# Rows of a routed layer fetched and stored by DMA through DRAM instead of one-hot products on TensorE, for seven of eight experts

## The reference

```python
N_EXPERTS_2, D_FF_EXPERT, TOP_K = 8, 3584, 2

def moe_swiglu(x, w_router, w_gate, w_up, w_down):
    logits = (x @ w_router).astype(jnp.float32)
    top_val, top_idx = lax.top_k(logits, TOP_K)
    top_w = jax.nn.softmax(top_val, axis=-1)
    gate = jnp.einsum('bsk,bske->bse', top_w,
                      jax.nn.one_hot(top_idx, N_EXPERTS_2, dtype=jnp.float32)).astype(x.dtype)
    y = jnp.zeros_like(x)
    for e in range(N_EXPERTS_2):
        h = jax.nn.silu(x @ w_gate[e]) * (x @ w_up[e])
        y = y + gate[..., e:e + 1] * (h @ w_down[e])
    return y

# second_block, layer i = 1, its last lines
ff = moe_swiglu(h, moe_w_router[j], moe_w_gate[j], moe_w_up[j], moe_w_down[j])
h = layer_norm(ALPHA_2 * h + ff, ln_g[i, 2], ln_b[i, 2])
```

## Time and profile before

| | us |
|---|---|
| median of three runs | 2299.82 (2298.18 to 2302.2) |
| the profiled execution | 2297.7 |
| its span (first to last instruction) | 2295.9 |
| the second routed layer, about 1256 to 2281 in the trace | 1025 |
| one expert within it | 125.6 |

### The profile page before, as it was taken

The page is one execution under the profiler, slowest core; times in us unless marked ns, Lnnn a source line. Parts: engine busy times, 40 slices in busy tenths (PEclk is TensorE's granted clock), DMA queues, the critical chain, the costliest instruction groups (busy, mean ns, idle before and its releaser), DMA issues.

```text
span 2295.9 us, 31086 instructions
## 1 busy us (share of the span) xinstructions
PE 2154.6 (94%) x12260; PEld 1728.6 (75%) x12260; DVE 1556.2 (68%) x1913; ACT 1226.8 (53%) x1352; POOL 127.4 (6%) x123
## 2 busy tenths in 40 slices
PE   8998899999988889999987999999999999999996
PEld 8886883443876879987676788888888888888885
DVE  4557661222556676763477888888888988888886
ACT  4554431111335454433555777776777777777773
POOL 2112000000000023330000000000000000000000
PEclk9998999999989999998999999999999999999998
DMA  8640649999452344567113899999999999999994
GB/s 268 185 147 3 191 177 385 417 417 408 144 170 86 103 164 165 168 194 183 65 56 129 306 369 332 366 334 363 347 351 346 352 355 347 367 330 367 335 368 155
DMA packets 285709, 592.02 MB, mean 258 GB/s; under 512 B 12155, under 2 KB 118031, under 8 KB 277280
## 3 DMA queue, kind: packets, MB, share of 16 engines
q1 hardware_dynamic: 280016, 571.54, 69.9%
q0 software_dynamic: 5584, 19.00, 2.7%
HBM read 589.39 MB, written 1.11 MB: 257 GB/s over the span
## 4 chain that ended last, share of the span: by engine, by line
PE 84%; DVE 6%; ACT 4%; DMA 3%; issue 2%; POOL 0%; SPq 0%; DVEq 0%; ACTq 0%
PE psF L1137 12%; PE psF L1139 12%; PE psF L1138 12%; PE psB L1137 9%; PE psB L1138 9%; PE psB L1139 9%; PE psF L1554 4%; PE psB L1576 2%; PE psB L1416 1%; PE psB L1599 1%; PE psF L1380 1%; PE psB L1211 1%; PE psF L1585 1%; DVE ring_rounded L2269 1%; PE psB L1219 1%
## 5 line engine op out<-in xcount | busy, mean ns | idle before, releaser
L2664 DVE TENSOR_TENSOR ring_rounded<-ring,arena_rounded 128x2048 fp32r<-128x2048 f32 x226 | 512.0, 2286 | 31.2 <-ACT arena_rounded L2009 30.1
L2009 ACT ACTIVATE arena_rounded<-ring 128x2048 fp32r<-128x2048 f32 x226 | 433.7, 1920 | 168.9 <-DMA ring<-in_moe_w_up_dram 108.5
L1137 PE MATMUL psF<-arena_rounded 128*128 128x512 f32 x896 | 358.1, 400 | 3.6 <-ACT arena_rounded L2031 1.6
L1139 PE MATMUL psF<-arena_rounded 128*128 128x512 f32 x896 | 354.3, 395 | 0.0
L1138 PE MATMUL psF<-ring_rounded,arena_rounded 128*128 128x512 f32 x896 | 352.9, 394 | 0.0
L2269 DVE TENSOR_TENSOR ring_rounded<-ring,ring_rounded 128x2048 fp32r<-128x2048 f32 (+1 forms) x71 | 154.0, 2170 | 171.0 <-ACT ring_rounded L1837 170.6
L1137 PEld LDWEIGHTS psF<-arena_rounded 128*128 128x128 f32 x896 | 168.8, 188 | 43.4 <-issue 5.0
L1139 PEld LDWEIGHTS psF<-arena_rounded 128*128 128x128 f32 x896 | 168.5, 188 | 39.1
L1138 PEld LDWEIGHTS psF<-ring_rounded,arena_rounded 128*128 128x128 f32 x896 | 168.7, 188 | 37.5
L1138 PE MATMUL psB<-ring_rounded,PT_rounded 128*128 128x512 f32 x448 | 177.0, 395 | 0.0
L1837 ACT ACTIVATE ring_rounded<-ring 128x2048 fp32r<-128x2048 f32 (+1 forms) x71 | 128.6, 1813 | 85.4 <-PE psF L1139 62.7
(11 more groups left out here) (453 smaller groups left out, 4532.3 us busy)
## 6 DMA issues: line engine op xcount, KB each, us to landing
ring<-in_moe_w_gate_dram SPq DMA_DIRECT2D x112, 1024.0 KB, 5.2
ring<-in_moe_w_up_dram SPq DMA_DIRECT2D x112, 1024.0 KB, 5.2
ring<-in_moe_w_down_dram SPq DMA_DIRECT2D x112, 1024.0 KB, 4.9
ring<-in_w_dram SPq DMA_DIRECT2D x48, 1024.0 KB, 16.7
arena<-in_w_dram SPq DMA_DIRECT2D x16, 1024.0 KB, 19.1
ring<-in_w_in_dram SPq DMA_DIRECT2D x14, 1024.0 KB, 5.3
ring<-in_ff_w_gate_dram SPq DMA_DIRECT2D x11, 1024.0 KB, 7.4
ring<-in_ff_w_up_dram SPq DMA_DIRECT2D x11, 1024.0 KB, 9.8
```

Of the source, the lines that this page charges most:

```text
L1137: mm(bank, x1, w1, start=start, stop=False, skip_group_check=open_groups)
L1139: return mm(bank, x2, w1, start=False, stop=stop, skip_group_check=open_groups)
L2009: ap_(w_hi[slot].bitcast(R32), ring[:, slot], ACT.Copy).then_inc(q["high"], 1)
L2664: V.tensor_tensor(ring_r[:, slot].bitcast(R32), ring[:, slot], w_hi[slot], ALU.subtract)\
```

## The change

For all units of round 0 (`direct` is true when the layer is split and the round is the number 0):
- The tokens `h` are written to DRAM once (1 MB). DVE computes for each token the numbers of its two slots (`number_rows`, step 3 of unit 0) and its gates (`gates_of_rows`, step 4). POOL scatters the token numbers to a table in DRAM with four indirect DMAs and reads it back as one column per expert.
- For units 1 to 7 POOL brings the rows with one indirect DMA of 128 rows of 4 KB into `xg_rows2`. PE's `gather` and ACT's `rows` are left out for them. `turn_rows` stands ahead of the last `down` of a unit instead of in its middle, and the halves of the rows (`slots`) come between the first and the second weight chunk on ACT and on DVE.
- For units 0 to 6 ACT copies the result without its gate (`y_save`) and POOL stores it to DRAM (0.5 MB each). `marks`, `y_high`, `y_low`, `scatter` and their sums are left out for them.
- In unit 7 POOL brings back, for each half of the tokens, two rows per token (four indirect DMAs of 0.5 MB), and DVE adds them with their gates in steps 3 and 5 (`add_rows`). Unit 7's own result goes the old way by `marks`, `y_high`, `y_low`, `scatter`.
- The counts on which semaphores are awaited are adapted, and two columns join the constants.

```diff
+        y_rows = Region(13824).get(D)
+        n_back = E2 - 1
+        tokens_dram = nc.dram_tensor("routed_tokens", (T, D), F32, kind="Internal").ap()
+        y_dram = nc.dram_tensor("expert_rows", (n_back * SLOTS, D), F32, kind="Internal").ap()
...
+            moe2 = layers["moe2"]
+            pool.wait_ge(numbers_ready, 1)
+            pool.dma_start(token_of[0:E2 * SLOTS].rearrange("(p e) a -> p (e a)", p=P), no_token).then_inc(blanked, 16)
+            pool.wait_ge(moe2.q["tokens_dve"], 1)
+            pool.dma_start(tokens_dram.rearrange("(t p) d -> p t d", p=P), h[:]).then_inc(tokens_out, 16)
+            pool.wait_ge(numbers_ready, 2)
+            pool.wait_ge(blanked, 16)
+            for k in range(2):
+                for t in range(TT):
+                    i = TT * k + t
+                    pool.indirect_dma_start(token_of, bass.IndirectOffsetOnAxis(slot_no[:, i:i + 1], 0), own_no[:, t:t + 1], None)\
+                        .then_inc(numbers_out, 16)
+            pool.wait_ge(numbers_out, 16 * 2 * TT)
+            pool.dma_start(token_no, token_of[0:E2 * SLOTS].rearrange("(e s) a -> s (e a)", s=SLOTS),
+                           allow_slow_non_contiguous=True).then_inc(numbers_back, 16)
+            pool.wait_ge(numbers_back, 16)
+            pool.wait_ge(tokens_out, 16)
+            def store_rows(u):
+                pool.wait_ge(y_saved, 2 * u + 2)
+                pool.dma_start(y_dram[SLOTS * u:SLOTS * u + SLOTS], y_rows).then_inc(y_out, 16)
+            for u in range(1, E2):
+                pool.wait_ge(moe2.q["slots_ready"], 2 * u)
+                pool.indirect_dma_start(xg_rows2, None, tokens_dram, bass.IndirectOffsetOnAxis(token_no[:, u:u + 1], 0))\
+                    .then_inc(rows_in, 16)
+                if u >= 2:
+                    store_rows(u - 2)
+            store_rows(n_back - 1)
+            pool.wait_ge(y_out, 16 * n_back)
+            pool.wait_ge(moe2.q["slots_ready"], 2 * E2)
+            for t in range(TT):
+                if t:
+                    pool.wait_ge(back_added, t)
+                for k in range(2):
+                    i = TT * k + t
+                    pool.indirect_dma_start(back_rows[:, k], None, y_dram, bass.IndirectOffsetOnAxis(back_no[:, i:i + 1], 0))\
+                        .then_inc(back_in, 16)
...
                 def down(u, s, n, where, next_rows=None):
                     pe.wait_ge(q["turned_dve" if layer.split else "turned_act"], steps_done + n)
-                    if s == 0:
-                        past(q["y_dve"], 2 * units_done + 2 * u)
+                    if s == 0 and direct:
+                        past(y_saved, 2 * u)
+                    elif s == 0:
+                        past(q["y_dve"], 2 * layer.written(r, u))
                     for j in range(2):
                         if j == 1 and next_rows is not None:
                             turn_rows(next_rows)
...
                 def turn_rows(u):
                     rows_ = xg_rows1 if per == 1 else xg_rows2
+                    brought = direct and not (isinstance(u, int) and u == 0)
+                    if brought:
+                        pe.wait_ge(rows_in, u * 16)
                     for a in range(2):
-                        pe.wait_ge(q["rows_saved"], (units_done + u) * 2 + 2)
+                        if not brought:
+                            pe.wait_ge(q["rows_saved"], layer.gathers(r, u) * 2 + 2)
                         for k in range(4):
...
-                    scattered = per == 1 and (isinstance(u, int) and u >= 2) or per > 1 and s == 1 and not begin
+                    scattered = per == 1 and (isinstance(u, int) and u >= 2) or per > 1 and s == 1 and not begin and not direct
                     if not begins:
-                        if s == 2:
+                        if s == 2 and not direct:
                             pe.wait_ge(q["added"], layer.adds(r, u, 0))
                         elif per == 1 and (u >= 2 or not (isinstance(r, int) and r == 0)):
                             pe.wait_ge(q["added"], layer.adds(r, u - 2, 0))
                         out_of = u - 1 if per > 1 else u - 2
                         scatter(out_of, steps_done + n)
                     gate_up(n, 1, 1, where)
-                    if per == 1 and not begin or per > 1 and s == 1:
+                    if per == 1 and not begin or per > 1 and s == 1 and (end or not direct):
                         mine = u if per > 1 else u - 1
                         if scattered:
                             pe.wait_ge(q["added"], layer.adds(r, out_of, 1))
                         marks(mine)
-                    if s == per - 1 and not end:
+                    if s == per - 1 and not end and not direct:
                         gather(u + 1, layer.adds(r, out_of, 3) if scattered else None)
                     next_rows = u + 1 if s == per - 1 and not end else None
+                    if direct and next_rows is not None:
+                        turn_rows(next_rows)
+                        next_rows = None
                     if not begins:
                         down(u if s else u - 1, (s - 1) % per, n, where, next_rows)
                     elif next_rows is not None:
...
+                def y_save(u, n, where):
+                    act.wait_ge(q["used"], layer.nth(layer.every, r, n, 6 * layer.group - 1, where))
+                    for c in range(2):
+                        ap_(y_rows[:, 512 * c:512 * c + 512], Y[c][:, :], ACT.Copy).then_inc(y_saved, 1)
                 def unit(u, begin, end):
                     for s in range(per):
                         step(u, s, begin and s == 0, end and s == per - 1, end)
+                    if direct and not begin:
+                        act.wait_ge(y_out, u * 16)
...
+                    switch = s == per - 1 and not end
                     if layer.split and not ends:
                         high(n + 1, 0)
+                    if switch and direct:
+                        slots(u + 1)
+                    if layer.split and not ends:
                         high(n + 1, 1)
-                    if s == per - 1 and not end:
+                    if switch and not direct:
                         rows(u + 1)
                     if layer.split and not ends:
                         high(n + 1, 2)
-                    if s == per - 1 and not end:
+                    if switch and not direct:
                         slots(u + 1)
                     if layer.split and not ends:
                         high(n + 1, 3)
                     if s == 0 and not begins:
-                        y_high(u - 1, n, where)
+                        (y_save if direct else y_high)(u - 1, n, where)
...
+                def number_rows():
...
+                    V.tensor_scalar(own_no, spare_row, -float(E2 * SLOTS + 1), None, ALU.add)
+                    do(V.tensor_scalar(slot_base, const("iota")[:, 0:E2], float(SLOTS), 1.0, ALU.mult, ALU.add))
+                    do(V.tensor_tensor(ids, slot, slot_base.unsqueeze(1).broadcast_to([P, TT, E2]), ALU.add))
+                    do(V.scalar_tensor_tensor(out=ids, in0=slot, scalar=SLOTS - 0.5, in1=ids, op0=ALU.is_lt, op1=ALU.mult))
...
+                    do(V.scalar_tensor_tensor(out=pairs(none_of), in0=pairs(two_ids), scalar=0.5,
+                                              in1=spare_row.unsqueeze(1).broadcast_to([P, 2, TT]), op0=ALU.is_lt, op1=ALU.mult))
+                    V.scalar_tensor_tensor(out=slot_no, in0=two_ids, scalar=-1.0, in1=none_of, op0=ALU.add, op1=ALU.add)
+                    V.tensor_scalar(back_no, two_back, -1.0, 0.0, ALU.add, ALU.max).then_inc(numbers_ready, 1)
...
+                def gates_of_rows():
...
+                    some, own = gates[:, :, 0:n_back], same[:, :, 0:n_back]
+                    V.tensor_reduce(gate_sum, some, AX.X, ALU.add)
+                    do(V.tensor_tensor(own, ids[:, :, 0:n_back], two_back[:, 0:TT].unsqueeze(2).broadcast_to([P, TT, n_back]), ALU.is_equal))
+                    do(V.tensor_tensor(own, own, some, ALU.mult))
+                    do(V.tensor_reduce(back_gate[:, 0:TT], own, AX.X, ALU.add))
+                    do(V.tensor_tensor(back_gate[:, TT:2 * TT], gate_sum, back_gate[:, 0:TT], ALU.subtract))
...
+                def add_rows(t):
+                    part = acc_of[layer.name][:, t]
+                    dve.wait_ge(q["added"], CREDIT)
+                    dve.wait_ge(back_in, 32 * t + 32)
+                    for k in range(2):
+                        i = TT * k + t
+                        ins = V.scalar_tensor_tensor(out=part, in0=back_rows[:, k], scalar=back_gate[:, i:i + 1], in1=part,
+                                                     op0=ALU.mult, op1=ALU.add)
+                        if k == 0:
+                            do(ins)
+                    ins.then_inc(back_added, 1)
...
+                    if direct:
+                        dve.wait_ge(back_added, TT)
...
```

(14 more changed lines are left out.)

64 lines of the change are left out of this document (50 added, 14 removed).

## The result

| | before | after |
|---|---|---|
| median, us | 2299.0 (2297.2 to 2302.2, 4 runs) | 2280.67 (2280.1 to 2285.41, 4 runs) |
| profiled execution, us | 2297.7 | 2281.02 (span 2279.2) |
| from the first gather matmul to the last turn, us | 1004.61 | 992.08 |
| one middle expert, us | 125.6 | 121.2 |

What follows compares the result with a forecast made beforehand. The prediction took TensorE (PE) to set the layer's pace. Savings of 30.4 us on PE, plus 1 for the move, minus 1 for DVE, took 2297.7 to 2267.3, forecast as a median of 2269 us, range 2263 to 2290.

Steps and rivals of the forecast that it cites:

- forecast case: Whole kernel: DVE's lead over PE covers the added work and bursts, giving 2264 to 2274 us; chance 0.69.
- rival 1: Routed layer: DMA engines give only 368 GB/s and take over, 2284 us; with bursts partly reaching PE, 2275 to 2290; chance 0.16.
- What leaves PE: Gather, scatter and marks leave PE seven times each: 13.0, 12.7 and 4.7 us, sum 30.4 us.
- The first gather's chain: Expert 0: scatters, reading back and gather land in time for PE; cost 0 us, ends 0 and 10.
- Rival 3: First gather late, or POOL starved writing descriptors: PE stands once at the transposes, up to 10 us, 2279; chance 0.05.
- The move of the transposes: Transposes ahead of the last down product: PE's wait for halves shrinks, 0 to 2.5 us saved, 1 taken.
- (a): DVE numbering rows in expert 0, step 3: 14 tiny operations, 2.8 us, exceeding the lead by 0.4 us.
- (b): DVE computing gates in expert 0, step 4: six operations, 1.2 us, before DVE has caught up wholly.
- Block (c): DVE's sums in the last expert, 2.4 us in step 3 and again in step 5, fit a 4.2 us lead.
- Room on the DMA side: Routed layer: engines can give 391 GB/s against a mean of 373 wanted, room of some 5%.
- Rival 2: Every expert DMA-bound below the present pace, turning point 359 GB/s; 2326 us at 351 GB/s; chance 0.07 for the region.
- Bursts: Each 0.52 MB row transfer delays a weight chunk by 1.35 us, covered by a 4.2 us lead; uncovered, 19 us.

Runs made afterwards that it cites:

- e1: The changed kernel without the four indirect scatters of token numbers and without the wait for them: 2271.34 us.
- e2: The changed kernel with table entries 64 bytes apart, each scattered number still 4 bytes: 2272.15 us.
- e3: The changed kernel with table entries 64 bytes apart and all 64 bytes written per number: 2269.36 us.
- e4: e3 with the transposes back in the middle of the last down product and the halves of the rows at their old places: 2289.03 us.
- e8: e3 with each expert's row gather and store done twice, and ACT making down chunk 5's high half after SiLU and turned values: 2267.85 us.
- e9: e3 with each expert's row gather and store done three times, and ACT making down chunk 5's high half after SiLU and turned values: 2277.09 us.
- b3: e3 with unit 7's sums spread over steps 2 to 5, and ACT making down chunk 5's high half after SiLU and turned values: 2266.61 us.

## Why the prediction was right, and where it was off

The direction and the main mechanism were right, and 2280.67 lies in the stated range. That it does is in part luck: it is outside the forecast case (2264 to 2274), in the region kept for rival 1, and what put it there was none of the rivals.

**What leaves PE: right.** 1.86, 1.81 and 0.67 us per expert. The step with the scatter and the marks went from 19.65 to 17.15, the change of unit from 20.2 to 18.03, and the six middle experts from 753.5 to 727.3 us: 26.2 against the 26.9 forecast with the move in it. The one exception is the marks of unit 0: only 0.23 us of 0.67 came, since PE then waited 0.60 us for the turned values.

**The first gather's chain: the term that failed.** I put down its waiting time, 0 with 0 and 10 as ends, and asked only whether it comes in time. It does: from 1331.03 to the landing of the gather 7.6 us after 1363.96 are 40.5 us, against the 44 that I had allowed and 47 that there were. What I never priced is what these DMAs do to the others. "No row shows an indirect transfer" stood there, and the bounds came from landing times, while the four scatters, 2 KB of numbers, cost 12.7 us in one step, above the upper end of 10. e1 shows the cause, e2 and e3 the property. Rival 3 had the expert and the size nearly right, one hole of up to 10 us, but the wrong mechanism and the wrong moment: the two holes end at 1347 and 1364, and PE never stood at the transposes, "near 1381", for rows.

POOL was held up by DVE, but it cost nothing. It issued a row gather in 1.0 to 1.5 us and a scatter in 1.9 to 2.8, and PE waited for no row gather. What DVE did beside the first scatter (1331.03, 2.83 us) and the first row gather (1363.96, 0.99 us):

```profile
1330.64 4.49 DVE L2802 TENSOR_TENSOR ring_rounded<-ring,arena_rounded 128x2048 fp32r<-128x2048 f32 x2
...
1363.43 0.68 DVE L2824 TENSOR_TENSOR arena<-arena,psF 128x512 f32<-128x512 f32 x1
```
The first row is two subtractions of 2.29 us whose inputs are both in SBUF. The first of them ends at 1332.93, and the scatter's issue 0.9 us later, at 1333.86. The other row has one input in PSUM, and the issue beside it was not held. So it is in all the traces: of 180 indirect DMAs whose issue began within a subtraction of two SBUF tensors, 179 ended it 0.8 to 0.9 us after the end of that subtraction, up to 3.0 us in all; the 49 others took 0.94 to 1.00. The plain stores of POOL took 0.56 to 0.60 in the midst of such subtractions. The Trainium skill, page "SBUF — State Buffer", section "Who interferes with whom", from which the prediction took that such a subtraction leaves POOL alone, also says that a DVE instruction with two SBUF inputs contends with a GpSimd instruction that reads SBUF. The traces agree with the latter for indirect DMAs, whose row numbers lie in SBUF, and with the former for the plain ones.

**The move of the transposes: right in sign, mis-sized in kind.** I compared it with the old kernel, where it is worth 0.36 us at most. In the new kernel, without the gather, it is worth 17.3 us (e4). My sum was not off by that, since both came together; but my reasoning called the gather pure cost, and it was cover too. Had the change been made in two steps, the first (e4) would have brought 9.5 us in the layer, and next to nothing of the 13.0 put down for the gather.

**DVE's blocks.** (a) and (b) lasted 2.3 and 1.1 us against 2.8 and 1.2, and cost PE nothing that can be seen: e1, e2 and e3 have all of it and a fourth step of 17.15 to 17.17. I had 1 us. "Block (c) fits" into a lead of 4.2 us: wrong. Two sums in a row are 2.60 us, close to the 2.4 put down, but the lead was shorter there. Without them the low half begun at 2195.20 could have begun at 2192.68 and been done at 2195.0; PE wanted it at 2196.5 (1.14 ahead of 2197.62). That is a lead of 1.5 us, not 4.2. DVE came to the turned values 5.2 us behind the turn (2189.87 against 2184.68), where the rows of the lead have 2.3 (1775.53 against 1773.23): it had waited for ACT, and ACT for chunks. That the burst of brought-back rows made these late is not shown by itself. Unit 7 is 3.6 us worse than forecast.

**Room on the DMA side: right.** The forecast set 391 GB/s against 373 wanted. The middle units ran at 373 with PE full, and with more traffic 381 and 386 were reached (e8, e9), 399 for 50 us. Rival 1, a ceiling of 368, would have given 2284, near the measured time, but for the wrong reason: no step of the middle experts but the changes of unit is above 17.8 us. Rival 2 had a turning point of 359. The rule of the Trainium skill that it leaned on, page "DMA: Bandwidth & Descriptors", section "Where 436 GB/s comes from", gives about 358 GB/s from HBM per core; 373 to 386 over 720 us do not agree with it. This program runs on one core; what the figure is worth with a second core loading, no run here shows.

**Bursts: half right.** "It delays a weight chunk by that much, against a lead of 4.2 us" holds for gate and up chunks. The lead at the down chunks is smaller, because ACT's work for PE's next product stood behind them. That costs the kernel after the small losses of 0.2 to 0.6 us in a step here and there, and b3 takes them away.

With the spaced table, the sums spread and ACT's order, the same change measures 2266.6: what the sum had said, 2269, was there to be had. ACT's order is not part of that sum, and no run has it in the kernel before; there plain steps are 17.14 to 17.17 us already, so it could give little.

## What to carry to other kernels

A small DMA has a second price beside its latency: what it does to the transfers of others while it is under way. Where no row shows such a transfer, bound that price from the weights it could hold up, and keep table entries written by an indirect DMA 64 bytes apart, the one distance tried here.

Work that is taken from the critical engine may have been the cover of another engine's work; look at who catches up during it, and move that work ahead in the same change.

A rate at which added traffic saturates is a ceiling only when nobody waits in a bad order. Look first at which tile the bound engine waits for; if it is not the loaded data, the order ahead of it is what to change.

## What the hardware showed that I had not expected

- Four indirect scatters of 4-byte numbers into neighbouring places in DRAM held the 16 engines at share 0.95 while they moved 152 to 216 GB/s, for some 25 us; the median landing of a weight chunk from 1325 to 1375 was 8.6 us (up), 13.1 (down) and 15.0 (gate), in e2 5.5 to 6.1. With entries 64 bytes apart: 351 to 364 GB/s.
- A PE hole costs more than itself. Behind 2.30 and 6.19 us of waiting the granted clock of the windows fell to 0.86 and 0.78, matmuls followed at 0.43 us for seven and nine intervals, and 8.5 us of waiting became 12.7.
- Weight loads with row gathers and stores among them kept 386 GB/s over 720 us and 399 over 50.
- An indirect DMA issued by POOL while DVE subtracts two SBUF tensors ends its issue 0.8 to 0.9 us after that subtraction (179 of 180 cases, up to 3.0 us instead of 0.94 to 1.00); a plain store of POOL is not held (0.56 to 0.60 us).
